# The oldest tap and the bias of three causal convolutions: from VectorE to ScalarE

## The reference

```python
def causal_dwconv(x, w, b):
    c = x.shape[-1]
    y = lax.conv_general_dilated(x, w[:, None, :].astype(x.dtype), window_strides=(1,),
                                 padding=[(S_CONV - 1, 0)], dimension_numbers=("NWC", "WIO", "NWC"),
                                 feature_group_count=c)
    return y + b
...
xbc = jax.nn.silu(causal_dwconv(xbc, conv_w[i], conv_b[i]))
xs, bm, cm = jnp.split(xbc, [S_INNER, S_INNER + S_GROUPS * S_STATE], axis=-1)
```

## Time and profile before

| What | Value |
| --- | --- |
| Time, median of 3 runs | 1681.77 us (1680.89 to 1685.76) |
| The profiled execution's own time | 1680.02 us |
| Its span, first to last instruction | 1678.3 us |
| Mean granted TensorE clock | 0.981 of 2.4 GHz |
| VectorE busy | 1050.1 us (63%), 1288 instructions |
| ScalarE busy | 729.3 us (43%), 880 instructions |
| GpSimd busy | 264.3 us (16%), 272 instructions |
| DMA | 270.85 MB, mean 161 GB/s |

### The profile page before, as it was taken

How to read it: one execution, slowest core, us unless ns; L and a number is a source line. 1 busy time by engine, 2 the same in 40 slices (tenths; PEclk the granted TensorE clock), 3 DMA queues, 4 the chain that set the end, 5 groups by cost and what they waited for, 6 DMA issues and landing times.

```text
span 1678.3 us, 24971 instructions
## 1 busy us (share of the span) xinstructions
PE 1612.6 (96%) x9888; PEld 1422.0 (85%) x9888; DVE 1050.1 (63%) x1288; ACT 729.3 (43%) x880; POOL 264.3 (16%) x272
## 2 busy tenths in 40 slices
PE   7999989999999999999999999899999999999997
PEld 5888788998999978888778888798999999788885
DVE  5544587777886645454665455877787765454445
ACT  5444434344345435343554444344344443544444
POOL 0000024455430000000000000355435300000000
PEclk9999989999999999999999999899999999999999
DMA  7555534454544555555555554254453455465551
GB/s 240 194 176 196 153 105 125 123 149 127 152 148 161 169 178 201 184 187 179 165 187 177 189 186 138 89 156 121 150 150 100 150 186 189 156 203 179 196 175 63
DMA packets 245236, 270.85 MB, mean 161 GB/s; under 512 B 12504, under 2 KB 226360, under 8 KB 245176
## 3 DMA queue, kind: packets, MB, share of 16 engines
q1 hardware_dynamic: 239472, 266.90, 49.5%
q10 hardware_dynamic: 5704, 3.13, 0.7%
HBM read 268.94 MB, written 1.05 MB: 161 GB/s over the span
## 4 chain that ended last, share of the span: by engine, by line
PE 83%; DVE 6%; issue 5%; POOL 3%; ACT 2%; DMA 0%; POOLq 0%; DVEq 0%; SPq 0%; ACTq 0%
PE bank L1291 26%; PE bank L1317 16%; PE bank L1319 16%; PE bank L1318 16%; DVE w_lo L768 2%; POOL R L426 2%; PE bank L1359 1%; PE bank L1465 1%; PE bank L1303 1%; PE bank L1304 1%; PE bank L1305 1%; PE bank L1635 1%; PE bank L1312 1%; PE bank L1547 1%; ACT w_hi L483 1%
## 5 line engine op out<-in xcount | busy, mean ns | idle before, releaser
L768 DVE TENSOR_TENSOR w_lo<-w_raw,w_hi 128x2048 fp32r<-128x2048 f32 x252 | 590.6, 2345 | 306.4 <-ACT w_hi L483 306.2
L483 ACT ACTIVATE w_hi<-w_raw 128x2048 fp32r<-128x2048 f32 x252 | 481.6, 1913 | 232.2 <-PE bank L1319 119.9
L1291 PE MATMUL bank<-u_hi,w_hi 128*128 128x256 f32 x1152 | 336.0, 292 | 2.5 <-DVE u_lo L803 2.5
L1291 PE MATMUL bank<-u_lo,w_hi 128*128 128x256 f32 x1152 | 331.0, 287 | 0.0
L1291 PE MATMUL bank<-u_hi,w_lo 128*128 128x256 f32 x1152 | 330.8, 287 | 0.0
L1291 PEld LDWEIGHTS bank<-u_hi,w_hi 128*128 128x128 f32 x1152 | 226.4, 197 | 7.4 <-issue 6.3
L1291 PEld LDWEIGHTS bank<-u_lo,w_hi 128*128 128x128 f32 x1152 | 226.5, 197 | 0.1
L1291 PEld LDWEIGHTS bank<-u_hi,w_lo 128*128 128x128 f32 x1152 | 226.2, 196 | 0.0
L398 POOL TENSOR_TENSOR rms<-var,m_half 128x2 f32<-128x2 f32 x11 | 7.7, 698 | 1084.3 <-DVE var L796 1071.1
L1317 PE MATMUL bank<-w_hi,u_hi 128*128 128x512 f32 x416 | 166.3, 400 | 5.9 <-DVE u_lo L803 4.3
L1317 PE MATMUL bank<-w_hi,ha_hi 128*128 128x512 f32 x416 | 164.9, 396 | 3.5 <-DVE w_lo L768 3.5
(11 more groups left out here) (259 smaller groups left out, 2579.9 us busy)
## 6 DMA issues: line engine op xcount, KB each, us to landing
w_raw<-in_w_ffn_dram SPq DMA_DIRECT2D x264, 512.0 KB, 4.3
w_raw<-in_w_in_dram SPq DMA_DIRECT2D x160, 512.0 KB, 4.6
w_raw<-in_w_branch_b_dram SPq DMA_DIRECT2D x32, 512.0 KB, 3.9
w_raw<-in_w_branch_a_dram SPq DMA_DIRECT2D x16, 512.0 KB, 4.0
w_raw<-in_w_out_dram SPq DMA_DIRECT2D x16, 512.0 KB, 4.2
w_raw<-in_w_ple_gate_dram SPq DMA_DIRECT2D x16, 512.0 KB, 4.2
y_feat<-in_w_ple_dram ACTq DMA_DIRECT2D x2, 1024.0 KB, 4.9
h<-in_x_dram SPq DMA_DIRECT2D x2, 512.0 KB, 4.9
```

Of the source, the lines that this page charges most:

```text
L483: a_.activation(whi[slot][:, :, :], raw[slot][:, :, :], ACT.Copy).then_inc(sem["w_hi"], 1)
L768: v_.tensor_tensor(wlo[slot][:, :, :], raw[slot][:, :, :], whi[slot][:, :, :].bitcast(F32), ALU.subtract).then_inc(sem["w_lo"], 1)
L1291: i = mm(o, w[slot][:, k, cs], x[:, k, :], start=(k + q == 0 and not seeded), stop=(k == KD - 1 and q == 2 and not seeded), skip_group_che ...
```

## The change

`conv` on VectorE loses its tap 0. A new helper `first_tap` on ScalarE makes it: it waits for the evac of the unit (semaphore evac) and for group_ready, runs two activations of the function Identity (scale: the filter's column of tap 0, bias: the filter's bias, both per-partition columns), one per tile of 128 x 256, and signals the new semaphore tap_done. VectorE waits for tap_done before tap 1. `first_tap` stands right before `tanh_conv` in ScalarE's order in all places. VectorE still passes its own wait `taken`, for its evac, before that. No DMA is added, moved or removed, and nothing on TensorE, GpSimd or SP is.

```diff
--- before.py
+++ after.py
@@ -241,7 +241,7 @@
             wsm_loaded p_loaded out_stored rows_done par_tr h_ready sq_ready var_ready rms_ready
              u_hi_ready u_lo_ready silu_done prod_done h1_hi_ready h1_ready small_done x_abs sp_exp
             dA_ready ea_ready cum_done cum_exp row_tr row_ready row_back tok_ready r_built seg_done exp_done
-            conv_done tanh_done cv_ready scores_done d_ready p_exp pm_ready sct_ready cb_done cbm_done
+            tap_done conv_done tanh_done cv_ready scores_done d_ready p_exp pm_ready sct_ready cb_done cbm_done
             btok_ready m_ready xtr_done xw_ready heads_done cst_ready num0_ready yi_done im_done st_ready
             inter_ready num1_ready nsq_ready hvar_ready hrms_ready hn_ready hnT_done y_ready zth_ready
             ha32_ready ha_hi_ready ha_ready group_ready group_free ysq_ready yb_hi_ready yb_ready yss_done
@@ -576,6 +576,15 @@
                     def scaled(p):
                         act.wait_ge(sem["evac"], lay * NE + g * GU + (p + RING + 1))
 
+                    def first_tap(i, p, buf, t0, dst):
+
+                        scaled(p)
+                        act.wait_ge(sem["group_ready"], G + 1)
+                        for q in range(2):
+                            ins = a_.activation(dst[:, q, :], xin[:, buf, q, 0:S], ACT.Identity,
+                                                bias=gcb[:, t0 + q:t0 + q + 1], scale=gcw[:, 0, t0 + q:t0 + q + 1])
+                        ins.then_inc(sem["tap_done"], 1)
+
                     def tanh_conv(i, dst):
                         act.wait_ge(sem["conv_done"], G * 3 + (i + 1))
                         a_.activation(cth[:, :, :], dst, ACT.Tanh).then_inc(sem["tanh_done"], 1)
@@ -602,6 +611,7 @@
                     step(1)
                     if first:
                         row_scale(lay, 1)
+                    first_tap(0, BC, 0, 0, bcv)
                     tanh_conv(0, bcv[:, :, :])
                     if first:
 
@@ -622,8 +632,10 @@
                         tk = bank[6][:, 0:24].rearrange("p (a h) -> p a h", a=6)
                         a_.activation(tokc[:, 0:2, :], tk[:, 0:2, :], ACT.Copy).then_inc(sem["tok_ready"], 1)
                         a_.activation(tokc[:, 2:6, :], tk[:, 2:6, :], ACT.Exp).then_inc(sem["tok_ready"], 1)
+                        first_tap(1, X01, 1, 2, xcv[:, 0:2, :])
                         tanh_conv(1, xcv[:, 0:2, :])
                     else:
+                        first_tap(1, X01, 1, 2, xcv[:, 0:2, :])
                         tanh_conv(1, xcv[:, 0:2, :])
                         score_exp()
                         decay(1)
@@ -631,6 +643,7 @@
                     step(4)
                     if first:
                         score_exp()
+                    first_tap(2, X23, 0, 4, xcv[:, 2:4, :])
                     tanh_conv(2, xcv[:, 2:4, :])
                     if first:
                         decay(1)
@@ -972,15 +985,12 @@
 
                     def conv(i, buf, tiles, dst):
 
-                        for j in range(SCONV):
+                        dve.wait_ge(sem["tap_done"], G * 3 + (i + 1))
+                        for j in range(1, SCONV):
                             for q, t in enumerate(tiles):
                                 src = xin[:, buf, q, j:j + S]
-                                if j == 0:
-                                    ins = v_.tensor_scalar(dst[:, q, :], src, gcw[:, 0, t:t + 1], gcb[:, t:t + 1],
-                                                           ALU.mult, ALU.add)
-                                else:
-                                    ins = v_.scalar_tensor_tensor(out=dst[:, q, :], in0=src, scalar=gcw[:, j, t:t + 1],
-                                                                  in1=dst[:, q, :], op0=ALU.mult, op1=ALU.add)
+                                ins = v_.scalar_tensor_tensor(out=dst[:, q, :], in0=src, scalar=gcw[:, j, t:t + 1],
+                                                              in1=dst[:, q, :], op0=ALU.mult, op1=ALU.add)
                                 if j < SCONV - 1 or q == 0:
                                     ch.add(ins)
                                 else:
```

## The result

The changed kernel takes 1697.25 us (median of 4 runs, 1694.56 to 1700.26) against 1681.67 us before (1680.89 to 1685.76). The ratio of the two is 1.0082, with a 95% interval of 1.0060 to 1.0103: **slower by 0.8%**, 13.8 us by the ratio. The profiled execution took 1694.62 us, 14.6 more than the one of before.

The account below looks back on a forecast made before the run. TensorE, busy for 96% of the span, was taken to bound the kernel. First groups' 5.0 us of waits plus 4.2 us of lower clock, 9.2 us on the median of 1681.77, gave 1691 us; range 1681 to 1701.

Parts of the forecast that it names:

- the first rival: Later groups lose too: GpSimd's late cs holds up VectorE before step 6; 8 to 12 us, 1699 to 1702; chance 0.17.
- The price of the tap: ScalarE's pair takes 1.07 us, evac to tap 1 takes 1.14 instead of 0.81: 0.33 us later per convolution finding ScalarE free.
- First groups: Each layer's first group: taps queue on ScalarE, conv 2 and cs come late; TensorE loses 2.5 us each, 5.0 in all.
- the clock: First groups, unit Z0: TensorE's longer idle time lowers its granted clock, costing 2.1 us per group, 4.2 for two layers.
- Later groups: Six later groups: conv 2's tap waits behind step 4, vtok slips 1.9 us, but costed at nothing; bounds -0.1 to +2.0 per group.
- the cover at the evac of Z0: Later groups: VectorE's 2.40 us of idle time before Z0's evac absorbs the 1.9 us slip, with 0.5 us left.
- the hold: Later groups: VectorE and GpSimd's cs delay each other 2.7 us near step 6; 1.3 to 2.0 us counted per group.
- one of the prediction's own signs of being wrong: TensorE showing a wait at hn_ready or for R over 3 us per group would show the prediction wrong.
- Only the wait, no lower clock: First groups lose 5.0 us by waiting alone, clock unchanged: 1686.5 us or less, no change by the bound; chance 0.23.
- Faster: Five later groups gain if conv 0 moves step 2 against GpSimd's long R: 17 us gained, 1674 us; chance 0.10.
- A table load: Identity needs another activation table, so each convolution on ScalarE pays loads of 1.28 us: about 1712 us; chance 0.03.

## Why the prediction was right, and where it was short

The forecast was slower, 1691 us with 1681 to 1701. Measured were 1697.25: the direction held, the time lies in the range, and 9.2 us were forecast where 13.8 came (10.1 to 17.3). The forecast's own terms reached only to 1695; that the measured time is inside the range is owed to the first rival, for which the range had been widened (to 1701, though its own figure ran to 1702).

- *The price of the tap.* 1.07 us for a pair and 1.14 for the gap were forecast, 1.09 and 1.16 measured, so 0.35 us per convolution and not 0.33. That the 0.8 us saved on VectorE are no gain held: its busy time fell by 17 us, and the time rose. It did not fall by 20, because 8.8 us came back at Z0's gate (7.6 us of busy time before, 16.4 after). Tap 0 had taken 20.4 us, and the subtractions for the low parts and xwe now take 5 us less. The remaining taps of conv 0 make up only 0.5 us of the difference (27.9 before, 28.4 after), though their median rose from 485 to 614 ns.
- *First groups.* The chain of tokc, tap, conv 1, step 4, exponential, tap, conv 2 and cs is in the trace in this order. 2.5 us per group were forecast, and 2.1 for the clock. The two groups grew by 4.2 and 4.7 us against 4.6. Counted from the norm's rows, the product of B and C starts 2.7 us later in layer 0 and 2.4 in layer 1. The wait itself is 3.7 us and not 4.2, since TensorE reaches it 1.0 and 0.6 us later and not 0.3, of which 0.4 is a new wait for VectorE's dA_lo ahead of it. From that product to the heads the chain takes 8.14 and 8.95 us, where it was 6.65 in both layers: 1.5 and 2.3 us for the clock, which was 0.66 and 0.50 in the 5 us after the wait. The sum of the profiles is 8.9 us, and by medians it is 8.1 us, against my 9.2. That each single term came so near is partly luck, for the fall of the clock is not fixed by the wait. The same 5 us in layer 1 of the kernel with conv 1's tap only (wait 3.7 us), then of the kernel with taps in later groups only (wait 1.8 us):

```profile
1100.90:1105.90 5.00, 4.94 (x42) 4.97 (x43) 2.62 (x2) 2.34 (x3) 3.40 (x1) 1.00 0.05 4
...
1092.00:1097.00 5.00, 5.00 (x29) 5.00 (x30) 2.62 (x2) 2.33 (x3) 2.92 (x1) 0.66 0.00 0
```

The first kept the full clock and lost nothing after the wait, the second lost 1.5 us. Over the 26 first groups of the 13 profiles, the stretch behind the wait was lengthened in 9 of the 10 groups with a wait of 3.5 us or more, and in 2 of the 16 with 2.7 or less.
- *Later groups: the step that failed.* I wrote that the cover at the evac of Z0 "holds by 0.5 us", and costed later groups at nothing. It did hold, by 0.66 us where 2.40 lay before. But I had given the first rival, what moves behind that cover, only 0.17. It came too, beside the forecast and not in its place. Z0's gate by line, before and after (ns, minimum/median/maximum, over all eight groups):

```profile
L1084 DVE SCALAR_TENSOR_TENSOR zs<-zth,zs x8: 678/680/2876, 277.6 to 1310.4; 128x512 f32<-128x512 f32 x8
...
L1094 DVE SCALAR_TENSOR_TENSOR zs<-zth,zs x8: 680/2870/2880, 280.9 to 1325.5; 128x512 f32<-128x512 f32 x8
```

VectorE in layer 0's first later group after the change, and GpSimd beside it:

```profile
335.90 2.71 DVE L992 SCALAR_TENSOR_TENSOR xcv<-xin,gcw,xcv 128x256 f32<-128x256 f32 x6 [2.67 <-ACT xcv L584]
...
343.20 0.69 DVE L981 TENSOR_TENSOR zs<-bank,rB 128x512 f32<-128x512 f32 x1 [0.66 <-PE bank L1301]
...
349.66 2.88 DVE L1094 SCALAR_TENSOR_TENSOR zs<-zth,zs 128x512 f32<-128x512 f32 x1
352.46 2.28 DVE L781 TENSOR_TENSOR w_lo<-w_raw,w_hi 128x2048 fp32r<-128x2048 f32 x1
...
362.16 2.28 DVE L781 TENSOR_TENSOR w_lo<-w_raw,w_hi 128x2048 fp32r<-128x2048 f32 x1
```

```profile
340.51 8.68 POOL L442 TENSOR_TENSOR seg<-seg,cbm 128x1024 f32<-128x1024 f32 x2 [8.33 <-DVE cbm L1025]
349.15 2.84 POOL L446 TENSOR_TENSOR cs<-cs,bcv 128x1024 f32<-128x1024 f32 x1
```

VectorE waits 2.67 us for conv 2's tap, which stands behind step 4. The mask of C B comes late and GpSimd's seg with it, so that cs now lies beside Z0's gate: 2.88 us, not 0.68. That is a hold of 2.2 us, just ahead of step 6, where I had named 2.7. The last line has no idle time before it; the 0.69 us of the earlier trace rows are used up. The rest reaches GpSimd at the next group's start and TensorE's waits for R: 3.0 us in that group, and in layer 1, from 1180 to 1250 us:

```profile
PE bank L1475 <- POOL R L426: 3.4, 3, 2.3
```

That is over 3 us, so one of the prediction's own signs of being wrong did appear. I had priced the hold at 1.3 to 2.0 us for each of six groups. By medians it is 3.5 us in all (1.2 to 5.9), 0.6 a group. It does not get through to TensorE every time: layer 0's last group, also behind a held gate, waits 2.3 us for R. 9.2 + 3.5 is 12.7, inside the measured interval.

- *The other rivals.* "Only the wait, no lower clock" is out: 0.77 in the stretch where 1.00 stood. "Faster" is out: each of the six later groups still has one of GpSimd's R at 2.66 us. "A table load" is out: ScalarE has 48 instructions more than before, the 48 activations and no load, and its busy time rose by 25 us, which 48 activations of some 0.6 us, overlapping by pairs, account for. The Trainium skill (ScalarE: Activation LUTs, Table sets) says that identity is in every set, and the trace agrees. The estimate of 586 ns for this activation, worked out from figures of the Trainium skill (ScalarE: Activation LUTs, What ACT_TABLE_LOAD costs), is near the medians of 592 and 603 ns. The rule of the Trainium skill that add and multiply belong on VectorE (ScalarE: Activation LUTs, Rules for kernel authors) agrees with the result, but its reason, the speed per element, is the smaller part here: from evac to tap 1 it is 1.16 us against 0.81, and most of the loss is the order.

What stays open is how much of the later groups' 3.5 us is wait and how much clock: the executions differ by several us there by alignment alone, and no kernel was made that holds one of the two fixed.

## What to carry to other kernels

When work moves to an engine with an in-order list, its price can be less its duration than what stands ahead of it in that list at the moment its input is ready. Give each moved instruction its own place, at the point where its input arrives; placing it right before its old successor cost 13.8 us here. With the taps earlier it was 5.9, and with cs off the path as well it was nothing. Where the old engine must wait for the result, the busy time it saves was worth nothing here, and a cover that survives with half a microsecond should be counted as spent for whatever is queued behind it.

## What was not expected

Single executions of the same kernel differ by some 3 to 10 us (before: 1678.2 to 1687.9 over 20 runs). The later groups of the profiles suggest where this comes from. An instruction of GpSimd that begins just after one of VectorE's long subtractions often lasts until that has ended, 2.66 us and not 0.61 for an R, and TensorE's wait and the clock follow. Later groups moved by up to 4 us in profiles of kernels in which nothing of that group had been edited, so a stage's length in one profile is no evidence for differences of this size.

One of these alignments is no chance. In layer 0's second later group, after the change, two of GpSimd's small copies in a row were held so, where before it was one:

```profile
373.56 2.26 POOL L416 COPY gdk<-dcol 128x4 f32 x1
375.76 2.26 POOL L417 COPY ghn<-par 128x2 f32 x1
```

A copy of 2 to 4 columns takes 0.2 us otherwise. Over the 13 profiles such a pair occurs nine times, each time in the group behind one in which Z0's gate was held, and never elsewhere. The changed kernel has three, and they are the groups with waits for R of 3.0, 3.4 and 2.9 us. So this is one way in which the later groups' loss gets to TensorE. It is not the only one, and not every hold takes it: 17 gates were held with a group behind them, eight of these stayed without a pair, and two of the eight (in the kernel with conv 2's tap only) had waits for R of 3.0 and 2.9 us all the same.
